# Deeper memory attention, gates made where they are used, and Horner's rule in the scan of a two-block model on one Trainium2 core

## The reference

```python
def memory_attention(q, mem_k, mem_v):            # in both layers of the first block, 4 heads of 64
    s = jnp.einsum('bshd,bmhd->bhsm', q * MEM_DH ** -0.5, mem_k)
    p = jax.nn.softmax(s, axis=-1)
    return jnp.einsum('bhsm,bmhd->bshd', p, mem_v).reshape(B, S, MEM_W)

def even_mixer(x, w_in, ...):
    dn_qkv, dn_ab, dn_gate, rk_in, rk_gate = jnp.split(x @ w_in, EVEN_SPLITS, axis=-1)   # dn_ab is 16 wide
    ab = dn_ab.reshape(bsz, seq, 4, DN_HEADS).transpose(2, 0, 3, 1)
    g = -jnp.exp(dn_a_log)[:, None, :, None] * jax.nn.softplus(ab[:2] + dn_dt_bias[:, None, :, None])
    beta = jax.nn.sigmoid(ab[2:])
    # delta rule in chunks of 64, forwards and backwards: a unit triangular system per chunk and head
    # rwkv7_scan, forwards and backwards, 8 heads of 64:
    #   state = state * w_t + (state @ a_t) b_t^T + v_t k_t^T;  y_t = state @ r_t
```

## Time and profile before

| | us |
|---|---|
| median of 3 runs | 6976.05 |
| fastest, slowest of them | 6958.89, 6981.98 |
| the profiled execution, its own time | 6989.38 |
| its span, first to last instruction | 6987.6 |
| mean granted TensorE clock | 0.881 |
| busy: PE, PEld, DVE, ACT, POOL | 5603.2, 3068.0, 2333.7, 1178.4, 301.6 |

### The profile page before, as it was taken

The page is one execution under the profiler, slowest core; times in us unless marked ns, Lnnn a source line. Parts: engine busy times, 40 slices in busy tenths (PEclk is TensorE's granted clock), DMA queues, the critical chain, the costliest instruction groups (busy, mean ns, idle before and its releaser), DMA issues. The chain is left out here.

```text
span 6987.6 us, 96082 instructions
## 1 busy us (share of the span) xinstructions
PE 5603.2 (80%) x39658; PEld 3068.0 (44%) x39658; DVE 2333.7 (33%) x3925; ACT 1178.4 (17%) x1918; POOL 301.6 (4%) x320
## 2 busy tenths in 40 slices
PE   7998858894986548688859989889558998867778
PEld 4554443332456425233334338888524444322233
DVE  2334310003205643100045365555442120443331
ACT  1222100001110020000023122222201110422111
POOL 0000000001010000000010000000000000211100
PEclk9998869996998757799969999999879999889989
DMA  2110155553133330654332243232231222467721
GB/s 103 36 36 31 60 200 203 220 199 129 48 110 102 111 120 26 244 218 184 146 100 84 80 135 67 53 70 53 73 114 39 57 71 82 145 228 260 254 103 63
DMA packets 559787, 813.87 MB, mean 116 GB/s; under 512 B 176648, under 2 KB 308104, under 8 KB 558920
## 3 DMA queue, kind: packets, MB, share of 16 engines
q1 hardware_dynamic: 491272, 629.25, 27.0%
q0 software_dynamic: 28544, 103.82, 4.2%
q10 hardware_dynamic: 39616, 75.51, 3.0%
HBM read 967.67 MB, written 209.26 MB: 168 GB/s over the span
## 5 line engine op out<-in xcount | busy, mean ns | idle before, releaser
L701 PE MATMUL op_acc<-op_w,op_m 128*128 128x512 f32 x1024 | 451.1, 601 | 63.1 <-DMA op_w<-in_w_out 63.1
L158 PE MATMUL hi_acc<-xT,hi_w 128*128 128x512 f32 x1024 | 445.6, 594 | 8.0 <-DMA hi_w<-in_odd_w_in 8.0
L701 PEld LDWEIGHTS op_acc<-op_w,op_m 128*128 128x128 f32 x1024 | 196.1, 193 | 304.8 <-issue 240.1
L158 PEld LDWEIGHTS hi_acc<-xT,hi_w 128*128 128x128 f32 x1024 | 193.4, 191 | 242.4 <-issue 234.1
L158 PE MATMUL ri_acc<-xT,ri_w 128*128 128x512 f32 (+1 forms) x576 | 253.8, 599 | 10.6 <-DMA ri_w<-in_even_w_in 10.6
L537 PE MATMUL na_acc<-xT,na_w 128*128 128x512 f32 x448 | 219.5, 638 | 40.0 <-DMA na_w<-in_na_w_in 34.0
L158 PE MATMUL di_acc<-xT,di_w 128*128 128x512 f32 x512 | 224.8, 598 | 8.4 <-DMA di_w<-in_even_w_in 8.4
L158 PE MATMUL mi_acc<-xT,mi_w 128*96 128x512 f32 (+1 forms) x512 | 224.3, 598 | 0.0
L3483 PE MATMUL le_gp<-le_g,xT 128*128 128x512 f32 x512 | 220.9, 592 | 0.0
L1183 PE MATMUL moe1e_g_ps<-moe1e_wg,moe1e_xb 128*64 128x512 f32 x768 | 178.9, 620 | 32.9 <-DMA moe1e_wu<-in_exp_w_up 25.7
L1183 PE MATMUL moe0e_g_ps<-moe0e_wg,moe0e_xb 128*64 128x512 f32 x768 | 173.2, 604 | 22.8 <-DMA moe0e_wu<-in_exp_w_up 15.3
(11 more groups left out here) (669 smaller groups left out, 8944.5 us busy)
## 6 DMA issues: line engine op xcount, KB each, us to landing
moe0e_wg<-in_exp_w_gate SPq DMA_DIRECT2D x48, 2048.0 KB
moe0e_wu<-in_exp_w_up SPq DMA_DIRECT2D x48, 2048.0 KB
moe0e_wd<-in_exp_w_down SPq DMA_DIRECT2D x48, 2048.0 KB
moe1e_wg<-in_exp_w_gate SPq DMA_DIRECT2D x48, 2048.0 KB
moe1e_wu<-in_exp_w_up SPq DMA_DIRECT2D x48, 2048.0 KB
moe1e_wd<-in_exp_w_down SPq DMA_DIRECT2D x48, 2048.0 KB
op_m<-scratch_mixedT SPq DMA_DIRECT2D x32, 512.0 KB, 8.8
op_w<-in_w_out SPq DMA_DIRECT2D x32, 512.0 KB, 9.9
```

Source lines behind the costliest of these rows:

```text
L158: mm = pe.matmul(self.acc[i % 2][0:n, h * BANK:(h + 1) * BANK], self.wbuf[i % 3][:, k, 0:n], self.rhs[:, k, h * BANK:(h + 1) * BANK], star ...
L701: mm = pe.matmul(acc[:, n % AHEAD, h * BANK:(h + 1) * BANK], m[:, k, n * P:(n + 1) * P], wb[:, k, h * BANK:(h + 1) * BANK], start=(k == 0) ...
```

## The change

- **memory_attention:** PE's turn n issues scores of n, transposes of n - 2, product of n - 3. `e`, `nm` and `rs` get a third buffer. DVE's turn: maxima of n, normalisation of n - 1 (`soften`), copy of n - 4 (`take`). ACT's turn: exponentials of n, copy of n - 2 (`keep`). In the product the loops over m and h change places.
- **the gates:** the stage dnab and the function project_tm go. `delta_inputs` loads the 16 columns as `wab`, and PE begins with 256 products: 64 tokens stationary, 8 columns moved, for 16 chunks, 8 parts and both directions, straight into the two halves of the partitions as `g` wants them. One copy by DVE takes them from PSUM. The four DMAs that read `ab` go.
- **Horner in the wide chain:** `UnitSolve` has levels 1 to 4 of `UnitInverse` and of level 5 only MT. Instead of the inverse, the right side is carried through: `rfirst` = R rz, then three times w = rfirst - MT w, the last of them is `ru`. The subtraction is DVE's. The delta chain stays as it is.

```diff
@@ memory_attention
-        e = s.sb("e", [P, 2, 2 * M])
+        e = s.sb("e", [P, 3, 2 * M])
+                def score(n):
+                    i, j = steps[n]
+                    pe.wait_ge(exps, max(n - 1, 0))
...
+                def turn(n):
+                    pe.wait_ge(probs, n + 1)
+                    pe.wait_ge(probs_T, max(n - 1, 0))
...
+                def mix(n):
+                    i, j = steps[n]
+                    pe.wait_ge(probs_T, n + 1)
+                    pe.wait_ge(kept, max(n - 1, 0))
+                    for m in range(2):
+                        for h in range(2):
...
-                for n in range(N + 1):
+                for n in range(N + 3):
                     if n < N:
...
+                        score(n)
+                    if 0 <= n - 2 < N:
+                        turn(n - 2)
+                    if n >= 3:
+                        mix(n - 3)
@@ memory_attention, vector
+                for n in range(N):
...
+                    if n >= 1:
+                        soften(n - 1)
+                    if n >= 4:
+                        take(n - 4)
+                soften(N - 1)
+                for n in range(N - 4, N):
+                    take(n)
@@ memory_attention, scalar
+                def keep(n):
+                    act.wait_ge(turned, n + 1)
+                    act.wait_ge(outs, max(n - 1, 0))
+                    act.activation(pt[:, n % 2], tp[:, n % 2], ACT.Copy).then_inc(probs_T, 1)
...
+                    act.wait_ge(turned, max(n - 2, 0))
...
                     if n >= 2:
+                        keep(n - 2)
+                for n in range(N - 2, N):
+                    keep(n)
@@ delta_inputs
+        wab = s.sb("wab", [P, xT.shape[1], 2, 2, HEADS])
+        abp = sp_[:, 0:NC * 2 * HEADS].rearrange("p (n k h) -> p n k h", n=NC, k=2)
@@ sync
+                sp.dma_start(wab[:].rearrange("p k a d h -> p k (a d h)"), w_ab.rearrange("(k p) f -> p k f", p=P)).then_inc(ab_loaded, 16)
                 rows.load(sp, 0)
...
-                    for k in range(2):
-                        sp.dma_start(g[r, :, k, :], av[:, d, k]).then_inc(g_loaded, 16)
@@ tensor
+                pe.wait_ge(ab_loaded, 16)
+                KD = xT.shape[1]
+                for n in range(NC):
+                    for k in range(KD):
+                        for d in range(2):
+                            mm = pe.matmul(abp[d * CK:(d + 1) * CK, n], xT[:, k, n * CK:(n + 1) * CK], wab[:, k, :, d, :],
+                                           start=(k == 0), stop=(k == KD - 1))
+                mm.then_inc(ab_made, 1)
                 for i in range(N + 2):
@@ vector
-                dve.wait_ge(g_loaded, 16 * 9)
+                dve.wait_ge(ab_made, 1)
+                link(dve.tensor_copy(g[:], abp))
+                dve.wait_ge(g_loaded, 16 * 5)
@@ new class
+class UnitSolve(UnitInverse):
+    PE, ACTS, DVES = 5, 3, 6
+    def tensor(self, pe, t, level):
...
+        pe.wait_ge(self.by_dve, t * self.DVES + 5)
...
+                mm = pe.matmul(self.pc[r, g, :], self.N[r, g, :], self.R[r, g, :], start=True, stop=True)
+        mm.then_inc(self.products, 1)
+    def vector(self, dve, t, level, link):
...
+        dve.wait_ge(self.products, t * self.PE + 5)
+        dve.tensor_copy(self.MT[:], self.pc).then_inc(self.by_dve, 1)
@@ two_scans, tensor
-                def r_u(t):
-                    pe.wait_ge(rinv.by_act, t * rinv.ACTS + rinv.ACTS)
+                def r_first(t):
+                    pe.wait_ge(r_z_ready, t + 1)
                     pe.sem_inc(rinv.passed, 1)
-                    tiles(rb[1], S(rinv.inv_T), S(rz)).then_inc(r_us, 1)
+                    tiles(rb[0], S(rinv.R), S(rz)).then_inc(r_firsts, 1)
+                def r_next(t, n):
+                    if n == 0:
+                        pe.wait_ge(rinv.by_dve, t * rinv.DVES + 6)
+                        pe.wait_ge(r_first_kept, t + 1)
+                    else:
+                        pe.wait_ge(r_ws, t * 2 + n)
+                    pe.sem_inc(rinv.passed, 1)
+                    tiles(rb[(1, 0, 1)[n]], S(rinv.MT), S(rfirst if n == 0 else rw)).then_inc(r_ms, 1)
...
                         for level in range(2, 9):
-                            rinv.tensor(pe, t, level)
+                            if level <= 5:
+                                rinv.tensor(pe, t, level)
+                            if level == 5:
+                                r_first(t)
+                            if level >= 6:
+                                r_next(t, level - 6)
                             inv.tensor(pe, t, level)
...
-                        r_u(t)
                         new(t)
@@ two_scans, scalar
-                            rinv.scalar(act, t, level)
+                            if level <= 3:
+                                rinv.scalar(act, t, level)
+                            if level == 5:
+                                act.wait_ge(r_firsts, t + 1)
+                                act.activation(rfirst[:], rb[0][:], ACT.Copy).then_inc(r_first_kept, 1)
                             inv.scalar(act, t, level)
-                        act.wait_ge(r_us, t + 1)
-                        act.activation(ru[:], rb[1][:], ACT.Copy).then_inc(r_u_ready, 1)
@@ two_scans, vector
+                def r_horner(t, n):
+                    dve.wait_ge(r_ms, t * 3 + n + 1)
+                    dve.wait_ge(r_first_kept, t + 1)
+                    out, sem = (ru, r_u_ready) if n == 2 else (rw, r_ws)
+                    dve.tensor_tensor(out[:], rfirst[:], rb[(1, 0, 1)[n]][:], ALU.subtract).then_inc(sem, 1)
...
-                        for level in (1, 2, 3, 4, 5, 7):
-                            rinv.vector(dve, t, level, link)
-                            inv.vector(dve, t, level, link)
+                        for level in range(1, 9):
+                            if level <= 5:
+                                rinv.vector(dve, t, level, link)
+                            else:
+                                r_horner(t, level - 6)
+                            if level not in (6, 8):
+                                inv.vector(dve, t, level, link)
```

More of the change, by code:

```diff
@@ L188, in __call__ @@
         self.eng.wait_ge(self.sem, self.base + self.n)
[L191 to L227, removed]
-            @block.scalar
-            def _(act):
-                with act.Fori(0, NB) as t:
-                    act.wait_ge(stored, t * 16)
-                    for n in range(NT):
-                        act.wait_ge(products, t * NT + n + 1)
-                        act.activation(obuf[:, n, :], acc[n % 2][:, 0:cblock], ACT.Copy).then_inc(copied, 1)
 def memory_keys(nc, mem, g, b, w_kv, ident, ident_in, mem_kT_out, mem_v_out, beside):
@@ new lines, in mix @@
+                def mix(n):
[3 more added lines that the diff above has]
+                    for m in range(2):
+                        for h in range(2):
+                            c0 = (2 * j + h) * DH
+                            mm = pe.matmul(op[h * DH:(h + 1) * DH, n % 2, 0:P], mem_v[:, m, c0:c0 + DH], pt[:, n % 2, 2 * h + m, :],
+                                           start=(m == 0), stop=(m == 1))
+                    mm.then_inc(outs, 1)
@@ L395, in take, with soften @@
                     dve.tensor_copy(o[:, j, i * P:(i + 1) * P], op[:, n % 2, 0:P]).then_inc(kept, 1)
-                for n in range(N):
-                    b = n % 2
-                    dve.wait_ge(scores, n + 1)
-                    link(dve.tensor_reduce(nm[:, b, :], sp_[:, b, :, 0:M], AX, ALU.max))
-                    dve.tensor_scalar(nm[:, b, :], nm[:, b, :], -SCALE, None, ALU.mult).then_inc(maxima, 1)
-                    if n >= 1:
-                        take(n - 1)
+                def soften(n):
+                    b = n % 3
                     dve.wait_ge(exps, n + 1)
@@ L2360, in two_scans @@
         pc = s.sb("pc", [P, 2, PAIRS])
[L2361 to L2362 removed]
+        rak, rrb, rrk, rbt, rkt, rvt, rz, rfirst, rw, ru, ry, rstate = (
+            s.sb(n, [P, U, CK]) for n in ("rak", "rrb", "rrk", "rbt", "rkt", "rvt", "rz", "rfirst", "rw", "ru", "ry", "rstate"))
         rb = [s.ps(f"r{i}", [P, U, CK]) for i in range(4)]
[L2364 removed]
+        rinv = UnitSolve(s, "rinv", U, blk, eye, [rb[0][:], rb[1][:], rb[2][:]])
         loaded = [s.sem(f"loaded{c}") for c in range(2)]
```

77 lines of the change are left out of this document (31 added, 46 removed).

## The result

The changed kernel took 6883.16 us in the median of 4 runs (6879.81 to 6897.85), the kernel before 6979.01 beside it (6958.89 to 6983.61): ratio 0.9872, 95% interval 0.9848 to 0.9897, 96 us less. Measured again later it was 6883.35 against 6991.8, ratio 0.9857 (0.9842 to 0.9872); the medians differ by 108 us, and the ratio stands for 100. The forecast was 6911: the time lies inside the range (6872 to 6945) and outside the forecast case's own range (6895 to 6925). It is rival B's number, 6882, and the range holds it because it was drawn wide enough to take in B.

The account below looks back on a forecast made before the run. Stages follow each other behind barriers: attention bound by a round trip, scans by PE. Gains of 29 (attention), 8.5 (gates) and 27 (scans), say 65 us, took the median 6976 to 6911; range 6872 to 6945.

Parts of the forecast that it names:

- the forecast case: Whole kernel: 65 us less, 6911 against the median, own range 6895 to 6925, chance 0.5.
- rival B: Memory attention: clock at 1.00 instead of 0.50, a call near 41 us, kernel 6882; chance 0.22.
- the ring: Old memory attention: one round trip a step, transposes, ACT's copy, product, DVE's copy, reciprocal and multiply, 4.18 us.
- 14.5 a call, 29 for two: Memory attention, three deep: PE bound at 3.38 us a step, a call 55.8 instead of 70.3; ends 0 and 58.
- 8.5 us were foreseen: Gates in di: products end 27.3 us after their start, so first tile starts earlier than the former 35.9.
- The price taken from `moe_found`: Gates' products: 0.053 us an instruction, from a stage with 48 columns moved at clock 0.50; 512 take 27.3 us.
- Rival D: Gates: the products don't pair, 19 us lost in place of 8.5 gained, 6938; chance 0.1.
- 27 us were foreseen: Scans, Horner in the wide chain: 1.7 us less for each of 16 steps; ends 6 to 37.
- The layout, hop by hop: Scan step from level 5: products and waits laid out in order, `r_end` 11.7 us after N x R.
- what was named late next: Scan step: the delta chain, formerly hidden behind the wide one; PE waits 0.75 us for its inverse before `new`.
- Rival C: Scans: the delta chain's hops set the step, gain 6 us in place of 27, 6932; chance 0.12.
- Rival E: Scans: moved loop code adds a pause and low-clock stretch each step, 88 us outweighing 65, 6999; chance 0.06.

Follow-up runs that it names:

- Experiment 7: The kernel before with only attention's products with the values moved one step back (scores n, transposes n - 1, products n - 2): 6975.99 us, ratio 0.9988.
- Experiments 11: The changed kernel with 18 unused transposes of the identity in front of the gates' 512 products: 6885.50 us, ratio 0.9848 to the kernel before.
- experiment 12: The changed kernel with the gates' 512 products laid between the 32 products of the di stage's first tile: 6916.88 us, ratio 0.9893 to the kernel before.
- experiments 6: The kernel before, old attention order, with 28 unused transposes of the identity while PE waits for the queries: 6959.27 us, ratio 0.9957.
- 9: The changed kernel with 28 unused transposes of the identity in front of each memory attention: 6857.22 us, ratio 0.9812 to the kernel before.
- experiment 1: The kernel before with the three-deep memory attention alone: 6932.49 us against 6993.43, ratio 0.9908.
- 10: The changed kernel with 28 unused transposes of the identity behind the last products of each memory attention: 6859.98 us, ratio 0.9819 to the kernel before.
- experiments 2: The kernel before with the gates' products moved into the stage of the delta inputs alone: 6967.47 us, ratio 0.9963.
- 3: The kernel before with the wider recurrence's solve by Horner's rule alone: 6960.47 us, ratio 0.9957.

## Why the prediction came out as it did

**What bounds the kernel.** That memory attention is a round trip was right, and at the low clock the ring was the one that I named: transposes, ACT's copy, product, DVE's copy, reciprocal. Experiment 7 took product and copy out of it, and the step went from 4.18 to 3.69. What the prediction doesn't have is a second ring, somewhat shorter at the low clock, over ACT's exponentials, which stand behind the copy. It held the step of experiment 7, and at the high clock, where a step stayed at 3.23 for 3.26. The cure for both is the depth, so the number took no harm.

**Memory attention, the step that failed.** The term "14.5 a call, 29 for two" rests on "So PE becomes the bound, at 3.38 if one group starts where the last ends", that is at clock 0.50. The low clock's step was right as far as it went (3.26); the clock wasn't. It rose 9 us into each call, a call took 36.1, and the term measured 68 in the trace, 61 in the time of the part alone. Rival B had the mechanism and 29 a call, 5 too few. A step takes 1.92 and not 2.1 (PE's 2.02 us of groups overlap a little), which is 3 of them; the 7.3 us for filling and emptying the pipe were too many, and B left out that the first 9 us run at the low clock. So B's 6882 against 6883 is in part luck: its term was 10 too small, and the difference of the medians, 96, is 8 below that of the traces. I gave B 0.22 on the strength of dnab, busy without a break at 0.50. Experiments 11 and 12 show that dnab was a fair witness for the gates only: their 512 instructions kept PE busy for 27 us, and 546 instructions for 62 us, at 0.50. Attention's groups move 128 and 256 columns, and the rise behind the transposes of mln was the nearer witness.

The Trainium skill (TensorE: Matmul & The Clock Gate, Part 4) holds that transposes don't count towards the full clock. The traces disagree, for float32: in experiments 6 and 9 nothing but transposes of the identity ran on PE, and the clock went from 0.50 to 1.00 between 4 and 6 us after the first. The Trainium skill's other rule, that a change of tiling mode drains the engine (TensorEngine Tiling (Array Packing), Key Properties), fits the estimate of 0.24 us a change in experiment 12.

**The third step of depth** was not weighed in the prediction. It is worth 40 us: without it a pause of 0.69 us a step stays, and the clock stayed low for one call and half of the other.

**The gates.** 8.5 us were foreseen. The first tile starts 27.4 us after the first product instead of 35.9, and over the stages 7.0 to 7.3 us are gained. The price taken from `moe_found` (0.053 us an instruction, 27.3 for all) was right to 0.1 us, and so was the low clock. Rival D is out. Timed alone the part gave 26 (the interval is 16 to 35); its trace shows a surplus only in stages that it doesn't touch.

**Horner.** 27 us were foreseen; the stage gave 28 and 31 in the two traces of the changed kernel, and 21 for the part alone. The pauses at the loop heads are no part of the 28: they add up to 34 us in both traces, before and after. The layout, hop by hop, ended at 11.7 us, the trace at 11.9, and what was named late next, the delta chain in front of `new`, is so (0.52 of wait, 0.75 foreseen). Rival C is out. Rival E asked whether the layout of the code moves the pauses. It does, and the stage with it, by 15 us up (experiment 1) and 18 to 20 us down (6, 9 and 10), far from the 88 it would need.

**The sum.** 29 + 8.5 + 27 became 68 + 7 + 28 in the trace, and 96 and 108 us in the two measurements. Only the first term was far off.

**Left open.** The clock of the old attention rose within the call in the traces of other kernels and in neither of before's own; what decides it wasn't found. The parts' times don't add up (61 + 26 + 33 = 120 for 96 and 108). The spans add up better, 52.6 + 17.5 + 39.8 = 109.9 for 104.2, and two effects nearly cancel in them. In experiments 2 and 3 the old attention ran 18 and 17 us shorter than in before, a gain that the whole kernel, with the new attention, can't have again. And the scans took 15 and 7 us longer than before in experiments 1 and 2, and 8 longer than in the whole in experiment 3. Together 35 - 30 = 5 us, about the surplus.

**A version ahead of both.** The changed kernel with 28 idle transposes in front of each attention: 6857.22, 134 us less than before, 26 less than the changed one. It owes most of this to where it puts the scans' code, so the number of transposes would have to be found anew after any other edit.

## What to carry to other kernels

When an edit closes PE's gaps in a stage that runs at the low clock, work out its time at both clocks, and take as witness for the clock a stretch of like products (columns moved, shapes) rather than any busy one. To deepen a pipeline, write down the whole ring with every queue that it passes, ACT's order included; with one pause left in each step the clock stayed low here for one call and half of another. A change of 0.3% in a kernel of this length may come of the place of a loop that the edit never touched, so look at the loop heads of untouched stages before a small gain is credited to its edit, and count the instructions in front of each pause.

## What the runs showed of the hardware that was not expected

- Twenty-eight float32 transposes of a 128 x 128 identity raised the granted clock from 0.50 to 1.00 between 4 and 6 us after the first. Eighteen, which end after 4.1 us, in front of the gates' products did not.
- The gates' 512 instructions of 8 columns kept PE busy for 27.4 us, and mixed with 32 instructions of 512 columns for 62.4 us, with the clock at 0.50 all the time.
- A change between products on 128 x 128 and on 128 x 64 weights cost an estimated 0.24 us in that mixture.
- The same loop body pauses once (3.1 us) or twice (2.8 and 2.1 us at the second head) by its place in the program: 797 against 817 us for 16 steps. Each pause ends 1.2 to 1.9 us after a 16 KB transfer of the instruction queue has landed, and the second moves by one matmul instruction for each one inserted ahead of the loop (27 to 9 for 18).
